# One decoder-trunk step on one core: the first loads and the modulation products in another order

## The chip, the cores and the metric

The kernel runs on one core of a Trainium2 chip. Its time is the device time of one execution in microseconds (us). TensorE (PE) multiplies and transposes, VectorE (DVE) and ScalarE (ACT) work on tiles, GpSimd (POOL) and SyncE (SP) here mostly issue DMAs.

## The reference

One inference step of a one-layer trunk, for a prompt of 1024 tokens and a sample group of 8 x 8 tokens (1088 tokens, width 1024). The part that matters here is its beginning, cut down:

```python
def post_norm_layer(x, c, w_mod_l, b_mod_l, ...):
    m = (jax.nn.silu(c) @ w_mod_l + b_mod_l).reshape(B, 6, 1, D)
    sh1, sc1, g1, sh2, sc2, g2 = [m[:, i] for i in range(6)]
    mix_out, new_state = mix_fn(x * (1 + sc1) + sh1)      # split_proj(h @ w_in), pooling, gating, attention
    x = layer_norm(ALPHA * x + (1 + g1) * mix_out, ln_g_l[0], ln_b_l[0])
    h2 = x * (1 + sc2) + sh2
    ff = moe(h2, router_w, router_b, wg, wu, wd)
    return layer_norm(ALPHA * x + (1 + g2) * ff, ln_g_l[1], ln_b_l[1]), new_state
```

The modulation `silu(c) @ w_mod` has six vectors of 1024 for each of nine rows of c. The first two (sh1, sc1) are needed before anything can be projected; the other four only after the projection. `rel_bias` gives a table of biases by distance, used by the attention.

## The kernel before

**Blocks.** The program is a sequence of blocks with a barrier between them: projection and compression (`block_projection`), attention, output projection, routing, experts, combination. Inside a block each engine has its own list of instructions, written out by hand, and semaphores (`wait_ge`) order the engines. Nothing schedules at run time. Only `block_projection` is changed.

**Modulation.** `w_mod` is 24 MB. It is loaded in twelve halves, 0 to 11 (`mod_load`, 2048 KB each; half n is rows 4*(n%2) to +3 of vector n//2). Halves 0 to 3 have buffers of their own. Halves 4 to 11 share one buffer, so that the load of half n waits until the products of half n-1 are done (`mod_half_done`), and the first of them waits until the weights of stage B, which lie in the same memory, have been split (`w_lo`). `mod_products(n)` (L329) is 16 fp32 multiplications with 32 output rows each, 32 records in the trace. `mod_vector` (DVE) adds the bias; `modulation_turn` (L620) transposes a finished vector, and a copy by DVE (L1042) puts it into `modT`, which every tile of x needs.

**Tiles of x.** There are nine: eight of 128 tokens and one of the 64 sample tokens. Two buffers are used in turn, so that `load_x(i)` waits for the transposes of tile i-2 (`xT_ready`). `transposes(i)` (L656) are eight PE transposes; ACT (`h_part`) and DVE (`h_values`) apply scale and shift, and the result is split into a high and a low fp32r part (L824, L826, L941).

**Stages.** PE runs `natural(n)` for n = 0 to 26 (L673): stage A (n = 0 to 8, 384 columns of `w_in`), stage B (n = 9 to 17, 408 columns), stage C (n = 18 to 26, 256 columns), tile n%9 each. The weights of a stage are loaded raw, then split into parts by ACT (L808) and DVE (L914). In stage A the transposes of tile i+2 follow `natural(i)`. `keys` (L684) and `gating` (L696) are small PE steps between them. Eight `group`s (L713) follow. `MOD_AFTER` says after which n the products of halves 4 to 11 stand.

**Bias table.** PE and DVE make a table of 8 rows by 1152. ACT stores it (L838) to DRAM sixteen times over, 8 x 16 x 1152 fp32, for loads much later.

**SP's queue** is in order: a load that waits holds every load behind it. It issues the halves, the tiles of x, the weights, and thirteen small loads (L496, L499, L500: scales, norms, pool state, page table and others; `small_in`, `pe_in`). `keep_busy` (L90) is a row of PE transposes of the identity without use for the result.

Of the kernel before, what the change touches and what calls it, by code (L numbers as in the profile page):

```python
# [30 lines left out]
KT = D // P  # L31
# [3 lines left out]
NT = NP_TILES + 1  # L35
# [3 lines left out]
PW = 256  # L39
WINDOWS = (2, 4, 8, 16)  # L40
PBUF = 15
HD, NKV, REP, NH = 64, 2, 4, 8
# [334 lines left out]
WIDTHS = (384, 408, 256)  # L377
CUTS = (3 * P, 3 * P, NP_TILES * P + NS - 6 * P)
N_GROUPS_T = 8
MOD_AFTER = {NT + 2: 4, NT + 4: 5, NT + 6: 6, NT + 8: 7, 2 * NT + 2: 8, 2 * NT + 4: 9, 2 * NT + 6: 10, 2 * NT + 8: 11}  # L380


def projection_weights(c):
# [32 lines left out]
def block_projection(c):  # L416
# [2 lines left out]
    projection_weights(c)  # L419
    c_n = c.view(MIX_, D)  # L420
    onehot, relb = c.view(KT_, TABW), c.view(KT_ + TABW, NH)
    tab = c.view(VS_, TABW)
    sgu_n = c.view(KVR_, 4, P)
    consts = c.view(CPH_, P + 2 * NS)
    trilT, blk64, rep8 = consts[:, 0:P], consts[:, P:P + NS], consts[:, P + NS:]
# [35 lines left out]
    with nc.Block() as block:  # L461
        @block.sync
        def _(sp):
# [9 lines left out]
            def load_w(n, at, width, dst, ks=slice(0, KT)):  # L473
                sp.dma_start(dst[:, ks, :], w_src[:, ks, at:at + width]).then_inc(c.w_in_in[n], 16)

            for n in range(3):
                mod_load(c, sp, n)
            load_x(0)
            mod_load(c, sp, 3)
            for h in range(2):  # L480
                load_w(h, KV0, WIDTHS[0], c.w_raw[0], slice(4 * h, 4 * h + 4))
            load_x(1)
            load_x(2)
            sp.wait_ge(w_lo, A_UNITS)
            load_w(2, KV0 + WIDTHS[0], WIDTHS[1], c.w_raw[1])
            load_x(3)
            for dst, src in (
                (c.pool_sc, bass.AP(tensor=t["pool_scale"].tensor, offset=0, ap=[[1, P], [P, 2]])),
                (c.lnv_g, row_broadcast(t["sgu_ln_g"], 0, PW)),
# [8 lines left out]
                lo = HD * (g % 2)  # L498
                sp.dma_start(c.sgu_b[lo:lo + HD, g // 2, :], row_broadcast(t["sgu_b"], g * P, P, HD)).then_inc(small_in, 16)  # L499
            sp.dma_start(c.pe_n[0:32, :], t["cmp_pe"][0].rearrange("s (c q) d -> (s c) (q d)", q=2)).then_inc(c.pe_in, 16)  # L500
            for i in range(4, NT):
                load_x(i)
            load_w(3, 2 * PW, PW, c.w_raw[2])
            sp.dma_start(share.rearrange("p m t -> p (m t)"), t["share"]).then_inc(share_in, 16)
            sp.wait_ge(w_lo, FIRST_UNIT[2])
            for n in range(4, 8):
                mod_load(c, sp, n)
            sp.wait_ge(z_ready, 2 * NT)
            sp.wait_ge(w_lo, GROUP_UNIT)
            load_w(4, 0, 512, c.pu_raw)  # L510
            for n in range(8, 12):
                mod_load(c, sp, n)
            sp.wait_ge(z_ready, 3 * NT)
            load_w(5, Q0, 512, c.q_raw)
# [92 lines left out]
        def _(pe):  # L607
# [52 lines left out]
            def natural(n):  # L660
                st, i = n // NT, n % NT
                T, at = tile_rows(i), i * P
                if n >= 2:
                    pe.wait_ge(*((z_act, n - 1) if n - 2 < 2 * NT else (z_dve, n - 1 - 2 * NT)))
                hi, lo = c.w_parts[st]
                units = (A_UNITS, B_UNITS, C_UNITS)[st]
                for k in range(KT):
                    if st == 0 and k % 4 == 0:
                        pe.wait_ge(h_lo, 2 * i + 1 + k // 4)
                    if i == 0 and k * units % KT == 0:  # L670
                        pe.wait_ge(w_lo, FIRST_UNIT[st] + k * units // KT + 1)
                    for left, right in ((0, hi), (0, lo), (1, hi)):
                        mm = pe.matmul(stage_bank(n)[0:T, 0:WIDTHS[st]], h_parts[left][:, k, at:at + T], right[:, k, :],  # L673
                                       start=(k == 0 and left == 0 and right is hi), stop=(k == KT - 1 and left == 1))
                mm.then_inc(z_ready, 1)
# [75 lines left out]
            bias_table()  # L751
            mod_products(c, pe, 1)
            gate_weights()
            keep_busy(c, pe, 7, 12)
            mod_products(c, pe, 2)
            sample_gate_weights()
            keep_busy(c, pe, 3, 16)
            mod_products(c, pe, 3)
            for v in range(2):
                modulation_turn(v)  # L760
            transposes(0)
            transposes(1)
            for n in range(3 * NT):
                st, i = n // NT, n % NT
                natural(n)
# [8 lines left out]
            for n in range(N_GROUPS_T):  # L774
                group(n)
                if n == 0:
                    gating(smp)
                if n == 1:
                    buffer_turn()
                if n == 4:  # L780
                    natural_pool()
                if n == 5:
                    pool_mix(0)
                if n == 6:
                    pool_mix(1)
# [5 lines left out]
        def _(act):  # L791
# [42 lines left out]
            act.dma_start(consts, t["cph1"]).then_inc(cph1_in, 16)  # L834
            act.wait_ge(c_in, 32)
            act.activation(c_n[0:9, :], c_n[0:9, :], ACT.Silu).then_inc(silu_done, 1)
            act.wait_ge(tab_done, 1)
            act.dma_start(c.tab_d, tab[0:NH, :].unsqueeze(1).to_broadcast([NH, TROWS, TABW])).then_inc(c.tab_out, 16)  # L838
            for u in range(4):
                part_high(u)  # L840
            act.wait_ge(modT_done, 2)
# [4 lines left out]
            for n in range(2 * NT):  # L846
                st, i = n // NT, n % NT
                T, s = tile_rows(i), i % 2
                z = stage_bank(n)
                act.wait_ge(z_ready, n + 1)  # L850
                if st == 0:
                    if i >= 2:
                        act.wait_ge(kv_out[s], 16 * 2 * (i // 2))
                        act.wait_ge(kT_ready, i - 1)
                    act.copy(kv_a[s][0:T, :], z[0:T, 0:WIDTHS[0]]).then_inc(z_act, 1)
                    if i + 2 < NT:
                        h_part(i + 2)
                    if 3 <= i < 3 + B_UNITS:
                        part_high(FIRST_UNIT[1] + i - 3)
                    continue  # L860
                if i >= 2:
                    act.wait_ge(kT_ready, n - 1)
                if i >= 6:
                    act.wait_ge(win_out[s], 16 * ((i - 4) // 2))
                if i == 0:
                    act.wait_ge(c.tab_out, 16)
                act.copy(c.vs[0:T, i, :, :, :].rearrange("p b g d -> p b (g d)"),
                         z[0:T, 0:512].rearrange("p (b w) -> p b w", b=2)[:, :, 0:P])
                act.copy(kv_b[s][0:T, :], z[0:T, P:2 * P])
                act.copy(c.gates[0:T, i, :], z[0:T, 3 * P:3 * P + 24]).then_inc(z_act, 1)  # L870
                if i in (3, 4):
                    part_high(FIRST_UNIT[2] + i - 3)
# [30 lines left out]
        def _(dve):  # L903
# [151 lines left out]
            for n in range(2 * NT):  # L1055
                st, i = n // NT, n % NT
                if st == 0 and i + 2 < NT:
                    h_values(i + 2)
                    for half in range(2):
                        h_low(i + 2, half)  # L1060
                if n >= 1:
                    keys_out(n - 1)
                if st == 0 and 3 <= i < 3 + B_UNITS:
                    part_low(FIRST_UNIT[1] + i - 3)
                if st == 1 and i in (3, 4):
                    part_low(FIRST_UNIT[2] + i - 3)
                if st == 1 and i == 5:
                    mod_vector(c, dve, 2)
            for i in range(NT):
                normed(i)  # L1070
                if i == 0:
                    keys_out(2 * NT - 1)
                if i >= 1:
                    gated(i - 1)
                if i == 1:
                    mod_vector(c, dve, 3)
                if i == 5:
                    mod_vector(c, dve, 4)
                if i in (6, 7):
                    part_low(GROUP_UNIT + i - 6)  # L1080
            for n in range(N_GROUPS_T):
                if n == 0:
                    mod_vector(c, dve, 5)
                    gated(smp)
                if n < 2:
                    for j, w in enumerate(CUTS):
                        pc = 3 * n + j
# [1819 lines left out]
```

## Time and profile before

| | |
|---|---|
| three runs, median | 1250.42 us (1245.3 to 1256.1) |
| profiled execution | 1253.85 us |
| its span in the trace | 1252.1 us |
| busy: PE, DVE, ACT | 1119.1, 731.7, 587.6 us |
| stage A on PE | 47.12 to 96.5 us |
| stage B on PE | 96.5 to 144.2 us |
| stage C on PE | to 188 us |
| granted PE clock, mean | 0.946 of full |

The profiled execution is 3.4 us over the median of the three runs. Times in a trace count from the start of the span. A row's bracket gives the idle time just before it and what ended it.

### The profile page before, as it was taken

The numbers are of one execution on the slowest core, as the hardware profiler recorded it, in microseconds if no ns is written. First come the engines' busy times: TensorE is split into PE (matmuls) and PEld (weight loads), VectorE is DVE, ScalarE is ACT, GpSimd is POOL, SyncE is SP. The second block draws the span as 40 slices with busy tenths as digits, with TensorE's granted clock in tenths as the row PEclk, the third lists the DMA queues.
The fourth block names the chain that finished last, engine by engine and source line by source line (L and its number), as shares of the span: only waits on it lengthen the run. The fifth ranks groups of instructions, "written<-read, shape, count | busy, mean of one in ns | idle before, by whom it ended". The sixth has DMA issues, their size and how long they took to land. (4 is left out here: it accounts for less than half of the span.)

```text
span 1252.1 us, 20501 instructions
## 1 busy us (share of the span) xinstructions
PE 1119.1 (89%) x7389; PEld 904.6 (72%) x7390; DVE 731.7 (58%) x1433; ACT 587.6 (47%) x1022; POOL 135.2 (11%) x203
## 2 busy tenths in 40 slices
PE   5699989998799999999889936999999999999844
PEld 3598879987666777778568725878888888888611
DVE  1461263243554777777676768885484588565157
ACT  0461100113465776766533235774475477555145
POOL 0212402010100000000000001020000011000061
PEclk9799999999997999999999967999999999999967
DMA  9645755054484300000343357996696599693488
GB/s 325 200 140 222 288 206 154 1 62 111 127 332 165 61 1 2 1 2 2 109 143 122 118 211 281 374 385 252 232 377 223 222 383 392 263 372 114 175 302 151
DMA packets 92343, 238.07 MB, mean 190 GB/s; under 512 B 8662, under 2 KB 18069, under 8 KB 92239
## 3 DMA queue, kind: packets, MB, share of 16 engines
q1 hardware_dynamic: 76153, 189.92, 43.2%
q0 software_dynamic: 10288, 31.20, 8.0%
q10 hardware_dynamic: 5830, 15.99, 3.6%
q8 instruction: 45, 0.74, 0.2%
q14 instruction: 27, 0.22, 0.1%
HBM read 199.04 MB, written 44.33 MB: 194 GB/s over the span
## 5 line engine op out<-in xcount | busy, mean ns | idle before, releaser
L2562 PE MATMUL psum<-w_hi,x_parts 128*128 128x512 f32 x736 | 239.7, 397 | 9.0 <-DVE x_parts L2681 9.0
L2674 DVE TENSOR_TENSOR w_lo<-raw,w_hi 128x2048 fp32r<-128x2048 f32 x95 | 213.3, 2286 | 44.7 <-ACT w_hi L2615 43.7
L2615 ACT CAST w_hi<-raw 128x2048 fp32r<-128x2048 f32 x90 | 167.6, 1914 | 29.3 <-DMA raw<-in_moe_w_gate 15.2
L2562 PEld LDWEIGHTS psum<-w_hi,x_parts 128*128 128x128 f32 x736 | 139.8, 190 | 39.8 <-issue 10.7
L2562 PE MATMUL psum<-w_lo,x_parts 128*128 128x512 f32 x368 | 144.7, 393 | 0.0
L2562 PE MATMUL psum<-w_hi,a_parts 128*128 x368 | 120.4, 399 | 4.0 <-DVE a_parts L2687 4.0
L1758 DVE CUSTOM_DVE_ANT_0 low<-psum,high 128x512 f32<-128x512 f32 (+5 forms) x172 | 92.2, 578 | 42.1 <-PE psum L1446 28.0
L1476 PE MATMUL psum<-keep,low 128*128 128x128 f32 (+1 forms) x556 | 95.0, 292 | 11.9 <-ACT high L1705 6.1
L1644 ACT ACTIVATE low<-low,high 128x640 f32<-128x640 f32 (+9 forms) x140 | 98.9, 709 | 9.9 <-DVE high L1758 9.6
L1671 ACT COPY high<-psum 128x512 f32<-128x512 f32 (+3 forms) x128 | 63.7, 502 | 81.5 <-PE psum L1476 81.3
L713 PE MATMUL psum<-h_hi,l_parts 128*128 128x384 f32 (+1 forms) x384 | 93.8, 327 | 0.0
L2037 PE MATMUL psum<-wo_parts,mix_parts 128*128 128x512 f32 x384 | 93.2, 399 | 0.0
L1476 PEld LDWEIGHTS psum<-keep,low 128*128 128x128 f32 (+1 forms) x556 | 60.9, 143 | 43.5 <-issue 28.7
L2037 PEld LDWEIGHTS psum<-wo_parts,mix_parts 128*128 128x128 f32 x384 | 72.1, 191 | 17.1 <-issue 2.1
L2562 PEld LDWEIGHTS psum<-w_hi,a_parts 128*128 128x128 f32 x368 | 69.8, 190 | 18.2 <-issue 4.2
L2562 PEld LDWEIGHTS psum<-w_lo,x_parts 128*128 128x128 f32 x368 | 69.8, 190 | 14.0
L1494 PE MATMUL psum<-high 128*64 128x128 f32 x1056 | 73.4, 283 | 0.0
L2562 PE MATMUL psum<-w_lo,a_parts 128*128 x184 | 72.2, 393 | 0.0
L713 PEld LDWEIGHTS psum<-h_hi,l_parts 128*128 128x128 f32 x384 | 67.4, 188 | 0.6 <-issue 0.4
L673 PE MATMUL psum<-l_parts,h_hi 128*128 128x384 f32 (+3 forms) x288 | 64.9, 316 | 1.5 <-DVE h_lo L941 1.3
L1446 PE MATMUL psum<-score_parts 64*128 64x512 f32 (+3 forms) x528 | 65.1, 371 | 0.0
L1494 PEld LDWEIGHTS psum<-high 128*64 128x64 f32 x1056 | 57.5, 139 | 10.4 <-issue 8.0
(384 smaller groups left out, 1734.6 us busy)
## 6 DMA issues: line engine op xcount, KB each, us to landing
raw<-in_moe_w_gate SPq DMA_DIRECT2D x16, 2048.0 KB, 11.5
raw<-in_moe_w_up SPq DMA_DIRECT2D x16, 2048.0 KB, 11.0
raw<-in_moe_w_down SPq DMA_DIRECT2D x16, 2048.0 KB, 10.8
top<-in_w_mod SPq DMA_DIRECT2D x8, 2048.0 KB, 8.0
y_d<-work ACTq DMA_DIRECT2D x24, 512.0 KB, 5.8
low<-in_w_mod SPq DMA_DIRECT2D x4, 2048.0 KB, 18.9
high<-in_x_prompt SPq DMA_DIRECT2D x16, 512.0 KB, 3.9
y_d<-high SPq DMA_DIRECT2D x1, 8192.0 KB, 23.8
```

Of the source, the lines that this page charges most:

```text
L673: mm = pe.matmul(stage_bank(n)[0:T, 0:WIDTHS[st]], h_parts[left][:, k, at:at + T], right[:, k, :], start=(k == 0 and left == 0 and right i ...
L713: mm = pe.matmul(piece_bank(pc)[:, 0:w], left[:, k, :], h_parts[right][:, k, toks], start=(k == 0 and left is hi and right == 0), stop=(k ...
L1446: mm = pe.matmul(c.bank(2 * g + q % 2)[:, 0:w * P], left[rows, j, :], right[rows, br, keys], start=n == 0, stop=n == 2)
L1476: mm = pe.transpose(turn_bank(what)[0:w, (k - 4 * m) * P:(k - 4 * m + 1) * P], pb[n % 3][:, g, k * P:k * P + w], c.ident)
L1494: mm = pe.matmul(c.bank(6 + br)[HD * g:HD * g + HD, j * P:(j + 1) * P], c.vs[:, k0 + k, br, g, :], pT[n % 2][:, g, k, :], start=(k == 0), ...
L1644: act.activation(x, x, ACT.Exp, bias=mx[:, at + g:at + g + 1], scale=-1.0, accum_out=sums[g]).then_inc(e_ev, 1)
L1671: act.copy(dst[:, 0:w], src[:, 0:w]).then_inc(r_act, 1)
L1758: dve.tensor_tensor_reduce(pb[n % 3][:, g, at * P:at * P + cols], c.bank(2 * g + q % 2)[:, 0:cols], bias, -1.0, least if m else 3e38, ALU. ...
L2037: mm = pe.matmul(c.bank(2 * (s % 2) + n), mixed[i % 2][l][:, k, :], wo[w][:, k, n * 512:(n + 1) * 512], start=(k == 0 and l + w == 0), sto ...
L2562: mm = pe.matmul(out, left[l][:, k * P:(k + 1) * P], w[:, bass.ds(at - o + k * step, 512)], start=n == 0, stop=n == len(steps) - 1)
L2615: act.copy(c.w_hi[:, at:at + PART // 2], c.raw[:, o:o + PART // 2]).then_inc(hi_done[p], 1)
L2674: dve.tensor_tensor(low, c.raw[:, o:o + PART // 2], c.w_hi[:, at:at + PART // 2].bitcast(F32), ALU.subtract).then_inc(c.lo_done[p], 1)
```

## The change

It does five things in `block_projection`, and moves no arithmetic.

1. SP's queue in the front: tile 0 of x is asked for before half 2, tile 1 between the two pieces of stage A's weights, and tiles 3 to 8 in a row. The thirteen small loads and `share` come after them, behind the load of stage C's weights.
2. The bias table is made in another place of SBUF, the memory of stage C's raw weights. Its store moves from the front of ACT's list to stage A, after `h_part(6)` (iteration i = 4). Therefore the load of stage C's weights now waits for `tab_out`, and a wait of ACT for it at the first tile of stage B is gone.
3. PE in the front: vector 0 is turned right after half 1, tile 0 is transposed after half 2, tile 1 in the middle of `natural(0)`. The rows of `keep_busy` are 12, 16 and then 24 long; before they were 12 and 16.
4. Products of halves 4 to 11: before after n = 11, 13, 15, 17, 20, 22, 24, 26; now after n = 9, 11, 13, 15, 17, 21, 24 and after group 0.
5. `mod_vector` 2, 3 and 5 on DVE are moved to follow them.

```diff
-MOD_AFTER = {NT + 2: 4, NT + 4: 5, NT + 6: 6, NT + 8: 7, 2 * NT + 2: 8, 2 * NT + 4: 9, 2 * NT + 6: 10, 2 * NT + 8: 11}
+MOD_AFTER = {NT: 4, NT + 2: 5, NT + 4: 6, NT + 6: 7, NT + 8: 8, 2 * NT + 3: 9, 2 * NT + 6: 10}
...
-    tab = c.view(VS_, TABW)
+    tab = c.view(MIX_ + 2 * KT * WIDTHS[1], TABW)
...
-            for n in range(3):
-                mod_load(c, sp, n)
+            mod_load(c, sp, 0)
+            mod_load(c, sp, 1)
             load_x(0)
+            mod_load(c, sp, 2)
             mod_load(c, sp, 3)
-            for h in range(2):
-                load_w(h, KV0, WIDTHS[0], c.w_raw[0], slice(4 * h, 4 * h + 4))
+            load_w(0, KV0, WIDTHS[0], c.w_raw[0], slice(0, 4))
             load_x(1)
+            load_w(1, KV0, WIDTHS[0], c.w_raw[0], slice(4, 8))
             load_x(2)
             sp.wait_ge(w_lo, A_UNITS)
             load_w(2, KV0 + WIDTHS[0], WIDTHS[1], c.w_raw[1])
-            load_x(3)
+            for i in range(3, NT):
+                load_x(i)
+            sp.wait_ge(c.tab_out, 16)
+            load_w(3, 2 * PW, PW, c.w_raw[2])
+            sp.dma_start(share.rearrange("p m t -> p (m t)"), t["share"]).then_inc(share_in, 16)
             for dst, src in (
...
-            for i in range(4, NT):
-                load_x(i)
-            load_w(3, 2 * PW, PW, c.w_raw[2])
-            sp.dma_start(share.rearrange("p m t -> p (m t)"), t["share"]).then_inc(share_in, 16)
             sp.wait_ge(w_lo, FIRST_UNIT[2])
-            for n in range(4, 8):
+            for n in range(4, 10):
                 mod_load(c, sp, n)
             sp.wait_ge(z_ready, 2 * NT)
             sp.wait_ge(w_lo, GROUP_UNIT)
             load_w(4, 0, 512, c.pu_raw)
-            for n in range(8, 12):
+            for n in range(10, 12):
                 mod_load(c, sp, n)
...
                 for k in range(KT):
+                    if n == 0 and k == 4:
+                        transposes(1)
...
             gate_weights()
-            keep_busy(c, pe, 7, 12)
+            modulation_turn(0)
+            sample_gate_weights()
+            keep_busy(c, pe, 3, 12)
             mod_products(c, pe, 2)
-            sample_gate_weights()
+            transposes(0)
             keep_busy(c, pe, 3, 16)
             mod_products(c, pe, 3)
-            for v in range(2):
-                modulation_turn(v)
-            transposes(0)
-            transposes(1)
+            modulation_turn(1)
+            pe.wait_ge(sguS_done, 1)
+            keep_busy(c, pe, 7, 24)
...
                     if i + 2 < NT:
                         h_part(i + 2)
+                    if i == 4:
+                        act.wait_ge(tab_done, 1)
+                        act.dma_start(c.tab_d, tab[0:NH, :].unsqueeze(1).to_broadcast([NH, TROWS, TABW])).then_inc(c.tab_out, 16)
```

PE in the front, from the products of half 1 to stage A. Where a line has two numbers, the first is the changed kernel's: L621/L620 turn a vector, L642/L641 make the sample's gate weights, L657/L656 transpose x. Before:

```order
L635 MATMUL psum<-keep,high 128x128 x3
L90 MATMUL psum<-keep 128x128 x12
L329 MATMUL psum<-low,top 32x256 [waits modw_in2]
L329 MATMUL psum<-low,top 32x256 x15
L641 MATMUL psum<-high 64x64 [waits sgu_done]
L641 MATMUL psum<-high 64x64 x3
L90 MATMUL psum<-keep 128x128 x16
L329 MATMUL psum<-low,top 32x256 [waits modw_in3]
L329 MATMUL psum<-low,top 32x256 x15
L620 MATMUL psum<-keep,top 128x128 [waits mods_ready]
```

The transposes of tiles 0 and 1 then stand before stage A. Now:

```order
L642 MATMUL psum<-high 64x64 x3
L90 MATMUL psum<-keep 128x128 x12
L329 MATMUL psum<-low,top 32x256 [waits modw_in2]
L329 MATMUL psum<-low,top 32x256 x15
L657 MATMUL psum<-keep,high 128x128 [waits tab_done,x_in0]
L657 MATMUL psum<-keep,high 128x128 x7
L90 MATMUL psum<-keep 128x128 x16
L329 MATMUL psum<-low,top 32x256 [waits modw_in3]
L329 MATMUL psum<-low,top 32x256 x15
L621 MATMUL psum<-keep,top 128x128 [waits mods_ready]
L621 MATMUL psum<-keep,top 128x128
L90 MATMUL psum<-keep 128x128 [waits sguS_done]
```

Between half 3 and stage A stand one turn and 24 transposes of the identity, where two turns and the 16 transposes of tiles 0 and 1 stood.

SP's queue in stage A and at the beginning of stage B. Before:

```order
L474 DMA top<-in_w_in 128x8x408 [waits w_lo]
L471 DMA high<-in_x_prompt 128x1024 [waits xT_ready]
L496 DMA high<-in_pool_scale 128x2x1
L496 DMA high<-in_sgu_ln_g 128x256
...
L500 DMA keep<-in_cmp_pe 32x128
L471 DMA high<-in_x_prompt 128x1024 [waits xT_ready] x4
L471 DMA high<-in_x_sample 64x1024 [waits xT_ready]
L474 DMA low<-in_w_in 128x8x256
L504 DMA high<-in_share 128x32
L314 DMA top<-in_w_mod 128x4x1024 [waits w_lo]
```

Now:

```order
L474 DMA top<-in_w_in 128x8x408 [waits w_lo]
L471 DMA high<-in_x_prompt 128x1024 [waits xT_ready] x5
L471 DMA high<-in_x_sample 64x1024 [waits xT_ready]
L474 DMA low<-in_w_in 128x8x256 [waits tab_out]
L491 DMA high<-in_share 128x32
L501 DMA high<-in_pool_scale 128x2x1
...
L505 DMA keep<-in_cmp_pe 32x128
L314 DMA top<-in_w_mod 128x4x1024 [waits w_lo]
```

The load of half 4 (the last row) now stands behind a wait for the table's store and behind all small loads.

PE in stage B, at the end of `natural(9)`. Before:

```order
L673 MATMUL psum<-b_parts,h_hi 128x408 x2
L673 MATMUL psum<-b_parts,h_lo 128x408
L684 MATMUL psum<-keep,high 128x64 [waits kT_evac,z_act]
L673 MATMUL psum<-b_parts,h_hi 128x408 [waits z_act]
L673 MATMUL psum<-b_parts,h_hi 128x408
```

Now:

```order
L676 MATMUL psum<-b_parts,h_lo 128x408
L687 MATMUL psum<-keep,high 128x64 [waits kT_evac,z_act]
L329 MATMUL psum<-top 32x256 [waits mods_ready,modw_in4]
L329 MATMUL psum<-top 32x256 x15
L676 MATMUL psum<-b_parts,h_hi 128x408 [waits z_act]
```

The two rows of L329 are the products of half 4; before they stood two tiles later.

## Rows read from the trace of the kernel before

**Rows 1.** The page, engines: busy time, share, instructions.

```profile
PE 1119.1 (89%) x7389; PEld 904.6 (72%) x7390; DVE 731.7 (58%) x1433; ACT 587.6 (47%) x1022; POOL 135.2 (11%) x203
```

**Rows 2.** Timeline of PE in the front: start, duration, instruction, [idle before].

```profile
19.50 1.47 PE L90 MATMUL psum<-keep 128*128 128x128 f32 x12
23.89 2.40 PE L329 MATMUL psum<-low,top 128*32 128x256 f32 x32 [2.91 <-DMA low<-in_w_mod]
27.27 3.67 PE L90 MATMUL psum<-keep 128*128 128x128 f32 x16
36.77 3.64 PE L329 MATMUL psum<-low,top 128*32 128x256 f32 x32 [5.83 <-DMA low<-in_w_mod]
47.12 0.62 PE L673 MATMUL psum<-l_parts,h_hi 128*128 128x384 f32 x2 [1.33 <-DVE h_lo L941]
51.85 1.03 PE L656 MATMUL psum<-keep,high 128*128 128x128 f32 x8
59.84 1.97 PE L656 MATMUL psum<-keep,high 128*128 128x128 f32 x8 [2.52 <-DMA high<-in_x_prompt]
```

**Rows 3.** Busy time in stretches; the share behind POOL's is the granted PE clock.

```profile
26.00:31.00 5.00, 4.94 (x28) 4.20 (x24) 0.42 (x1) 0.00 (x0) 0.00 (x0) 0.50 1.01 278
41.00:45.00 4.00, 3.34 (x17) 3.31 (x17) 1.60 (x6) 0.81 (x3) 2.05 (x4) 0.50 0.09 23
46.00:57.00 11.00, 9.67 (x56) 9.11 (x56) 9.74 (x22) 8.08 (x19) 4.27 (x9) 1.00 0.60 197
```

**Rows 4.** DMA totals of 0 to 24 and of 19 to 22.5 us.

```profile
DMA packets 2896, 8.04 MB, mean 335 GB/s; under 512 B 270, under 2 KB 1038, under 8 KB 2895
...
DMA packets 366, 1.43 MB, mean 408 GB/s; under 512 B 20, under 2 KB 20, under 8 KB 365
```

**Rows 5.** DMA by queue, 22.5 to 33.5 us (q10: ACT's), then 33.5 to 43 us.

```profile
q10 hardware_dynamic: 136, 0.59, 35.1%
...
q1 hardware_dynamic: 799, 1.80, 52.1%
```

**Rows 6.** Timeline: ACT's store of the table, DVE's copy of vector 1, ACT in tile 6.

```profile
18.51 0.87 ACTq L838 DMA_DIRECT2D tab_d<-high  x1
...
42.42 0.23 DVE L1042 COPY keep<-psum 128x72 f32<-128x72 f32 x1 [0.78 <-PE psum L620]
...
79.91 0.62 ACT L826 CAST h_hi<-high 128x512 fp32r<-128x512 f32 x1
```

**Rows 7.** Timeline of SP's queue in stage A.

```profile
52.13 0.43 SPq L496 DMA_DIRECT2D high<-in_pool_scale  x1
...
60.15 12.84 SPq L471 DMA_DIRECT2D high<-in_x_prompt  x4
...
78.35 0.59 SPq L474 DMA_DIRECT2D low<-in_w_in  x1
```

**Rows 8.** DMA issues of 50 to 56, 92 to 102 and 112 to 121 us: KB, us to landing.

```profile
high<-in_x_prompt SPq DMA_DIRECT2D x1, 512.0 KB, 8.4
...
top<-in_w_mod SPq DMA_DIRECT2D x1, 2048.0 KB, 9.1
...
top<-in_w_mod SPq DMA_DIRECT2D x1, 2048.0 KB, 7.6
```

**Rows 9.** Timeline of PE at the end of `natural(9)`.

```profile
101.13 0.27 PE L684 MATMUL psum<-keep,high 64*128 64x64 f32 x1
```

**Rows 10.** Waits of PE from 90 to 300 us: total, times, longest.

```profile
PE psum L329 <- DMA top<-in_w_mod: 4.5, 4, 1.8
```

**Rows 11.** Timeline of PE and DVE at the end of stage C.

```profile
187.47 0.66 PE L696 MATMUL psum<-high 128*64 128x128 f32 x8
188.75 1.93 PE L329 MATMUL psum<-top 128*32 128x256 f32 x32 [0.63 <-DMA top<-in_w_mod]
190.62 0.62 PE L713 MATMUL psum<-h_hi,l_parts 128*128 128x384 f32 x2
...
189.52 0.54 DVE L974 TENSOR_SCALAR high<-psum,high 64x256 f32<-64x256 f32 x1
```

More of the change, by code:

```diff
@@ L777, in _ @@
                     gating(smp)
+                    mod_products(c, pe, 11)
                 if n == 1:
@@ L836, in _ @@
             act.activation(c_n[0:9, :], c_n[0:9, :], ACT.Silu).then_inc(silu_done, 1)
-            act.wait_ge(tab_done, 1)
-            act.dma_start(c.tab_d, tab[0:NH, :].unsqueeze(1).to_broadcast([NH, TROWS, TABW])).then_inc(c.tab_out, 16)
             for u in range(4):
@@ L864, in _ @@
                     act.wait_ge(win_out[s], 16 * ((i - 4) // 2))
-                if i == 0:
-                    act.wait_ge(c.tab_out, 16)
                 act.copy(c.vs[0:T, i, :, :, :].rearrange("p b g d -> p b (g d)"),
@@ L1066, in _ @@
                     part_low(FIRST_UNIT[2] + i - 3)
-                if st == 1 and i == 5:
+                if st == 1 and i == 4:
                     mod_vector(c, dve, 2)
+                if st == 1 and i == 8:
+                    mod_vector(c, dve, 3)
             for i in range(NT):
@@ L1074, in _ @@
                     gated(i - 1)
-                if i == 1:
-                    mod_vector(c, dve, 3)
                 if i == 5:
@@ L1082, in _ @@
                 if n == 0:
+                    gated(smp)
+                if n == 1:
                     mod_vector(c, dve, 5)
-                    gated(smp)
                 if n < 2:
```

## The prediction

> **What bounds the kernel now.** I read the page's engines first: PE is busy 89% of the span [rows 1], so what counts is where PE stands idle or at half clock, and the change touches only the first 200 us. Then PE's timeline in the front. It waits 2.91 us for half 2 of the modulation and 5.83 us for half 3, stage A begins at 47.12, and PE waits once more, 2.52 us, for tile 3 of x at 59.84 [rows 2]. The clock comes next: at half from 26 to 31 and from 41 to 45, full from 46 [rows 3]. After 60 us nothing is idle on PE until stage C, where it waits four times for a half, 4.5 us in all [rows 10]. So the block is a late start, one gap in stage A, four small ones in stage C, and otherwise back-to-back PE work. The changed kernel does the same PE work plus 24 transposes of the identity.
>
> I make the sum against the profiled execution, 1253.85 us, and set it off against the median of 1250.42, 3.4 us lower, at the end.
>
> **Why half 3 is late.** ACT issues the table's store at 18.51 [rows 6]. Its 0.59 MB take 35.1% of sixteen engines for 11 us [rows 5], which is 62 engine-us, against 1.43 MB in 3.5 us at 408 GB/s (56 engine-us for more than twice the bytes) just before [rows 4]. And once it is through, from 33.5 to 43 us, the loads use only 52.1% of the engines [rows 5]: about half of them have finished, and the other half still owe what they could not move while they stored the table. A load has landed when its slowest engine has.
>
> **Front, with the store gone.** By 24 us 8.04 MB were moved [rows 4]. Up to and with half 3 the queues carry four halves (8.4 MB), tile 0 (0.5) and about 0.8 MB of constants, 9.7 in all. The table had some 0.2 MB of the 8.04, so that 1.9 MB are left, 4.7 us at 408 GB/s: half 3 lands at about 28.7 and not at 36.8. Tile 0 now goes ahead of half 2 and delays it by 0.52 MB, 1.3 us: 25.2.
>
> PE then runs half 2, eight transposes of tile 0, 16 of the identity, half 3, one turn. At full clock these are 1.93 [rows 11], 1.03, 16/12 of 1.47 [rows 2], then 1.93: half 3 is begun at 30.1 and done at 32.0. At half clock they are 3.64, 1.97, 3.67 and 3.64 [rows 2]: done at 38.1. From the end of half 3's products to DVE's copy of vector 1 (42.42 to 42.65 [rows 6]) the old kernel took 2.2 us with two turns, the new one needs about 1.7. From that copy to stage A it took 4.5 us, of which 1.5 went to waiting for tile 0's transposes, which are now done before: 3.0. Stage A would start at 36.7 at full clock. The gap before half 2 is 2.5 us or so, and after gaps of 2.91 and 2.52 us the old kernel was at half clock [rows 2, 3]. [...] Gain **8.1** (7 to 10.4).
>
> **Tile 3 of x.** Its load lands 8.4 us after issue, in the company of 1632 KB of weights and small loads [rows 8]. Without the small ones (0.6 MB up to there) it lands 1 to 1.4 us earlier against the start of stage A, and PE arrives 1.03 us later, since the transposes of tile 1 now stand in `natural(0)` [rows 2]. Of the 2.52 us 0 to 0.5 are left, the clock doesn't fall, and the transposes at 59.84 cost 1.03 and not 1.97. Against it stand the 1.03 of tile 1. Gain **2.1** (1.5 to 2.5). Tiles 4 to 8 were not waited for before and are now asked for earlier.
>
> **The new wait in stage B.** The load of half 4 is now the last of a chain on SP. Count from ACT's cast of tile 6, behind which the store is issued: 79.91 in old time [rows 6], called T. The store took 11 us of transfer and at most 15.0 from issue to the end (18.51 to 33.5 [rows 5, 6]); with an idle queue I take 12.5 (11 to 15). Then SP issues stage C's weights and `share`, 1.2 us at 0.6 each, and the thirteen small loads, 8.0 us (52.13 to 60.15 [rows 7]): T+21.7. A half then needs 7.6 to 9.1 us [rows 8], I take 8.2: **T+29.9**. PE asks for it behind `keys(8)`, 101.4 in old time [rows 9], T+21.5. So PE waits **8.4** us (6 to 12), and since both ends hang on the same tile this doesn't depend on what the front gains. Behind the wait on PE stand all of stages B and C; nobody fills in. After so long a gap PE is at half clock: at least the products cost 3.64 and not 1.93, 1.7 us; at most it lasts as from 36.77 to 45.7, 9 us at half, 4.5 us. I take **2.5**. The other small costs have cover: the weights of stage C are asked for at T+12.5 and used in tile 12 of stage B, over 20 us later; the stores of k and v share the table's engines until T+12.5, and the first copy that waits for one of them is due about then.
>
> The Trainium skill (SBUF — State Buffer, on Door 1, the DMA port swizzle, with the port rate of DMA: Bandwidth & Descriptors, Where 436 GB/s comes from) lets eight neighbouring partitions reach only two of the sixteen ports, which for 0.59 MB gives an estimate of 10.8 us wherever the store stands; by that rule the 11 us of the row stay with it in stage A.
>
> **Products after that.** Half n is loaded once n-1 is done, 7.6 to 9.1 us; products two tiles of stage B apart are over 11 us apart, so no further wait. In stage C there are two products where there were four, three and four tiles apart: three waits go, 3.9 of the 4.5 us. The fourth was 0.63, at 188.75, and half 11's products stood there; now group 0 comes straight away, but it waits for DVE's `z_dve`, 189.52 + 0.54 = 190.06, against PE free at 188.13 [rows 11]. PE thus idles 1.9 us where wait and products took 2.5, and pays the products, 1.9 us, after group 0: 1.3 lost. Gain in stage C **2.5** (2 to 3.5). The page loads, behind product 11 on SP, start some 12 us later and are used over 60 us later.
>
> **Sum.** -8.1 - 2.1 + 8.4 + 2.5 - 2.5 = -1.8: 1252.0 for the profiled execution, **1249** against the median. Own range: -8 to +5, 1242 to 1255. Everything behind the block only shifts.
>
> **Rivals.**
> 1. *The table's store is cheap where it stands now*, with no other load in its way, or SP's small loads go out faster: no wait in stage B, clock kept. For it: alone, it may not need 11 us. Against: half 4 would have to be asked for 14 us after T, and 9.2 us of issues alone lie before it. -12.7: 1238. Chance 0.12.
> 2. *Slower: PE stays at half clock through the front.* Place: PE between half 2 and stage A, where 24 transposes of the identity now stand. For it: from 26 to 31 us PE was busy almost throughout, 16 such transposes among it, and stayed at 0.50 [rows 3]. Against: it was at 0.50 from 41 to 45 with the transposes of tiles 0 and 1 and at 1.00 from 46 [rows 3]. Price: half 3 done at 38.1, turn at 39.4, the 24 at 3.67/16 each 5.5 us, stage A at 44.9 and not 39, part of it given back at tile 3: +5.3, 1254. It decides from a start of stage A later than 41, where the gain of the front no longer pays the wait in stage B. Chance 0.13. The Trainium skill (TensorE: Matmul & The Clock Gate, Part 4: PE-mode transpose) says that transposes don't count as activity that lifts the clock. By that rule rival 2 is what happens; the rows from 41 to 57 us speak against it.
> 3. *The change doesn't do what it says in the front*: half 3 lands at 36.8 as before, because something else held it. Stage A at 43.5 to 45; the rest as above: +3.5, 1252.5. The half-idle engines [rows 5] speak against it. Chance 0.08.
>
> **How the numbers follow.** Forecast 0.67, rivals 0.12, 0.13, 0.08. About 1%, 12.5 us, is what a measurement of this kernel tells from no change; the forecast and rivals 2 and 3 lie within it. Faster by more: most of rival 1 at its edge, 0.08. Slower by more: rival 2 together with the upper bounds of the wait, 0.05. The range is 1239 to 1257.
>
> **What the changed kernel's profile would show.** Half 3's products begin at 30 to 34.5 us; stage A at 36.7 to 40; the row of PE for tile 3 with under 0.5 us of idle; one wait of PE of 6 to 12 us for the load of half 4 after `natural(9)`, with half clock behind it; no wait at L329 in stage C. The prediction is wrong if that wait is missing or if stage A begins after 41.

## The result and the profile after

The changed kernel took **1255.11 us** (median of 20 runs, 1250.83 to 1258.35), the kernel before 1248.01 (20 runs). The ratio is 1.0049, 95% interval 1.0035 to 1.0064: 6.1 us slower by the ratio (7.1 by the medians). The forecast was 1249, within a microsecond or so of no change.

The two profiled executions hide this (spans 1252.1 and 1253.1 us), because the one of before ran 21 us of its attention block at half clock and the one of after did not. Busy time in 373 to 394 us, of before, then of after; the share behind POOL's is the granted clock:

```profile
373.00:394.00 21.00, 21.00 (x159) 12.76 (x148) 7.74 (x34) 9.14 (x32) 0.61 (x1) 0.51 0.49 160
```

```profile
373.00:394.00 21.00, 20.27 (x231) 13.77 (x232) 10.14 (x43) 13.28 (x47) 0.61 (x1) 1.00 0.70 224
```

So places in the program are compared, not spans. PE's timeline of the kernel after, front to first group (start, duration, instruction, [idle before]):

```profile
23.89 1.93 PE L329 MATMUL psum<-low,top 128*32 128x256 f32 x32 [1.41 <-DMA low<-in_w_mod]
26.69 1.91 PE L90 MATMUL psum<-keep 128*128 128x128 f32 x16
30.46 1.93 PE L329 MATMUL psum<-low,top 128*32 128x256 f32 x32 [1.86 <-DMA low<-in_w_mod]
33.22 2.78 PE L90 MATMUL psum<-keep 128*128 128x128 f32 x24
37.06 0.62 PE L676 MATMUL psum<-l_parts,h_hi 128*128 128x384 f32 x2 [1.06 <-DVE h_lo L945]
...
49.55 1.09 PE L657 MATMUL psum<-keep,high 128*128 128x128 f32 x8 [1.84 <-DMA high<-in_x_prompt]
...
84.86 0.61 PE L676 MATMUL psum<-b_parts,h_hi 128*128 128x408 f32 x2
...
107.83 3.22 PE L329 MATMUL psum<-top 128*32 128x256 f32 x32 [18.06 <-DMA top<-in_w_mod]
...
193.94 0.59 PE L716 MATMUL psum<-h_hi,l_parts 128*128 128x384 f32 x2 [2.08 <-DVE high L978]
```

Against [rows 2], stage A starts 10.1 us earlier and half 3 lands at 30.4 us instead of 36.7. Stage B begins at 84.86, in the kernel before at 96.50:

```profile
96.50 0.61 PE L673 MATMUL psum<-b_parts,h_hi 128*128 128x408 f32 x2
```

That is 11.6 us of lead. One wait of 18.06 us, for half 4, takes it and more. The first group starts at 193.94 and not at 190.62 [rows 11], 3.3 us late, and product 11 (1.93 us) is still to come. From stage B's start to the first group the kernel needs 15.0 us more: 18.06 of wait, +1.3 for the product at half clock, -4.5 for stage C's old waits [rows 10], -1.9 for product 11, +2.1 for the wait on DVE in the last row. The pool step, in both the same wait of PE on ACT, shows what then remains. After, then before:

```profile
270.44 3.45 PE L748 MATMUL psum<-high 64*64 64x512 f32 x12 [2.07 <-ACT high L899]
```

```profile
265.28 2.05 PE L745 MATMUL psum<-high 64*64 64x512 f32 x12 [2.07 <-ACT high L895]
```

It starts 5.2 us late and takes 1.4 us more, because in this execution the clock falls at that point (0.61 granted from 270 to 274 us): 6.6 us, against 6.1 measured.

**Why 18 us.** The queues of ACT, SP and POOL in the kernel after, in order of time:

```profile
67.76 0.87 ACTq L863 DMA_DIRECT2D tab_d<-low  x1
...
81.97 0.38 SPq L474 DMA_DIRECT2D low<-in_w_in  x1
...
87.42 0.60 POOL L587 DMA_DIRECT2D out_o_win_s<-in_state_win_kv  x1
...
90.60 20.91 SPq L314 DMA_DIRECT2D top<-in_w_mod  x2
```

The chain that I had worked out is there: 14.2 us for the table's store (12.5 foreseen), 8.6 us of issues (9.2 foreseen). New is the third row: GpSimd's copy of the window state, one array of device memory to another. Now it is 3 us ahead of half 4; in the kernel before it stood 7 us behind it (half 4 issued at 92.30):

```profile
99.05 0.60 POOL L586 DMA_DIRECT2D out_o_win_s<-in_state_win_kv  x1
```

DMA issues and queues in 90.6 to 108 us (KB, us to landing; the row DMA is the busy share of sixteen engines in 40 slices, in tenths):

```profile
DMA  0392999585599595977030234455555555420000
q1 hardware_dynamic: 804, 2.21, 34.1%
q0 software_dynamic: 65, 1.65, 23.5%
top<-in_w_mod SPq DMA_DIRECT2D x1, 2048.0 KB, 17.2
```

Half 4 needs 17.2 us from issue to landing, against the 7.6 to 9.1 of [rows 8]. From 98 to 106 us the engines are at most half busy (share 0.38, then 0.49), while half 4 has still not landed: the picture that [rows 5] gave of the table's store.

### The profile page after: what moved, and what is told of

It is laid out like the page before. It is cut to its first block and busy times, and to the rows that moved or that the text cites. A ratio compares the mean times of both kernels' runs of the same rounds, so it can differ in the third digit from the quotient of the medians.

```text
span 1253.1 us, 20548 instructions
## 1 busy us (share of the span) xinstructions
PE 1110.9 (89%) x7413; PEld 898.9 (72%) x7414; DVE 731.8 (58%) x1433; ACT 587.6 (47%) x1022; POOL 135.7 (11%) x203
## 5 line engine op out<-in xcount | busy, mean ns | idle before, releaser
L1649 ACT ACTIVATE low<-low,high 128x640 f32<-128x640 f32 (+9 forms) x140 | 98.9, 710 | 11.1 <-DVE high L1763 10.9
```

Of the source, the lines that this page charges most:

```text
L1649: act.activation(x, x, ACT.Exp, bias=mx[:, at + g:at + g + 1], scale=-1.0, accum_out=sums[g]).then_inc(e_ev, 1)
```

## The experiments

Ratios are against the kernel before, run beside each. "Wait" is PE's for half 4 and half 5 in stage B, from the profiled execution; "group 0" is the start of the first group there.

| kernel | median us | ratio (95%) | wait 4 / 5 | group 0 |
|---|---|---|---|---|
| before | 1248.0 | 1 | 0 / 0 | 190.6 |
| changed | 1255.1 | 1.0049 (1.0035 to 1.0064) | 18.1 / 0 | 193.9 |
| copy late | 1248.4 | 0.9987 (0.9966 to 1.0007) | 8.4 / 0 | 187.4 |
| half 4 first | 1249.9 | 0.9999 (0.9981 to 1.0017) | 0.3 / 9.2 | 187.0 |
| both | 1237.1 | 0.9892 (0.9866 to 0.9919) | 0 / 2.4 | 180.5 |
| store early | 1253.8 | 1.0036 (1.0013 to 1.0059) | 0 / 5.9 | 191.5 |
| copy, b c e | 1255.1 | 1.0044 (1.0024 to 1.0065) | 17.3 / 0 | 193.3 |
| before + places | 1254.8 | 1.0045 (1.0023 to 1.0067) | 0 / 6.6 | 193.7 |
| front only | 1250.0 | 1.0011 (0.9987 to 1.0034) | 9.4 / 0 | 190.2 |
| both, half 5 too | 1236.0 | 0.9886 (0.9855 to 0.9917) | 0 / 0.2 | 174.9 |
| copy in 62 | 1269.9 | 1.0153 (1.0123 to 1.0184) | 17.8 / 5.2 | 210.4 |
| before + places, copy late | 1245.8 | 0.9976 (0.9954 to 0.9998) | 0.5 / 0 | 185.0 |
| before, copy late | 1246.9 | 0.9973 (0.9952 to 0.9993) | 0 / 0 | 192.9 |
| the same again | 1251.2 | 1.0008 (0.9977 to 1.0039) | 0 / 0 | 191.4 |
| half 5 too, old places | 1239.3 | 0.9909 (0.9873 to 0.9944) | 0 / 0 | 180.7 |
| copy in 32 | 1255.0 | 1.0042 (1.0009 to 1.0074) | 13.9 / 0 | 193.0 |
| half 5 too, copy in 32 | 1237.5 | 0.9899 (0.9867 to 0.9932) | 0 / 0 | 176.1 |

Waits and group 0 are of one execution each, and those of copy late (1264.3 us) and of both (1241.5 us) are the longest of their kernels: in both of them stage B starts 1.9 us later than in the changed kernel's.

**Copy late.**

```diff
-            pool.dma_start(t["o_pool_s"][0, :, 0:PBUF - JS, :], t["state_pool"][0, :, JS:PBUF, :]).then_inc(c.out_done, 16)
-            pool.dma_start(t["o_win_s"][0, :, 0:PAST - JS].rearrange("b s a g d -> b (s a g d)"),
-                           t["state_win_kv"][0, :, JS:PAST].rearrange("b s a g d -> b (s a g d)")).then_inc(c.out_done, 16)
-            c.out_total += 32
...
             pool.dma_start(t["o_sgu_s"][0].rearrange("b j w -> (b j) w"), c.vn[smp % 2][0:NS, :]).then_inc(sgv_out, 16)
+            (the same four lines)
```

> The changed kernel with one edit: GpSimd's two copies from one array of device memory to another (pool state and window state, 1984 KB in eight long rows) are issued behind the last store of stage C, at about 192 us, instead of at 87.4 us. Theory (the copy stretched the landing of half 4): half 4, asked for at about 90.6 us, lands in 8 to 9 us instead of 17.2, TensorE's wait for it in stage B falls from 18.1 us to about 9, and the time falls by 8 to 10 us against the changed kernel, to about 1246 us. Rival (the landing is slow because of the table's store and the small loads of stage C's weights ahead of it on SyncE): the landing stays at 16 to 18 us and the time within 2 us of the changed kernel. Second rival: the copy has to be somewhere, and costs the same between 192 and 205 us, where half 11 or stage C's outputs are moved: wait gone in stage B, new one of 5 us or more behind it.

Half 4 was issued at 92.16. PE's timeline, then the DMA issues from 90 to 103 us:

```profile
100.06 3.64 PE L329 MATMUL psum<-top 128*32 128x256 f32 x32 [8.44 <-DMA top<-in_w_mod]
```

```profile
top<-in_w_mod SPq DMA_DIRECT2D x1, 2048.0 KB, 7.9
```

The landing falls from 17.2 to 7.9 us and the wait to 8.44, the 8.4 of the prediction. By the ratios the edit is worth 0.6%, 7.7 us. Both rivals fall: from 190 to 300 us PE waits for no half. (The profiled execution had 47 us at half clock in its attention block; only its first 200 us are used.)

**Half 4 first**, and **both** edits together.

```diff
+            sp.wait_ge(w_lo, FIRST_UNIT[2])
+            mod_load(c, sp, 4)
             sp.wait_ge(c.tab_out, 16)
...
-            sp.wait_ge(w_lo, FIRST_UNIT[2])
-            for n in range(4, 10):
+            for n in range(5, 10):
```

> The changed kernel with one edit: SyncE asks for half 4 as soon as its buffer is free, before it waits for the table's store and issues stage C's weights and small rows. Theory (chain of table store, 14.2 us, and SyncE's issues, 8.6 us, holds half 4 back, and the copy then stretches it): half 4 is issued near 80 us and landed near 88.5, TensorE asks for it at 89.7 and waits for nothing; half 5 then is the one behind the chain and beside the copy, issued near 91.8, landed near 107, asked for at about 101, wait 5 to 7 us. Time 11 to 13 us below the changed kernel, about 1242 us. Rival (half 4 is late for a reason of its own: its buffer or its own size): wait for half 4 stays above 8 us and the time moves by less than 4 us.

> The changed kernel with both edits: half 4 asked for first, and the two copies behind stage C's last store. Theory: no wait of TensorE for halves 4 or 5 in stage B; the time is 17 to 20 us below the changed kernel, about 1236 us, which would be 11 to 12 us below the kernel before. Rival (the waits of stage B are cover for something that ends as late, such as VectorE's work between stages): stage B is shorter but the first group starts at the same point, and the time falls by less than 10 us.

Half 4 first: its wait is gone, but half 5 is waited for 9.2 us, not 5 to 7, and the gain is 6 us, half of what I expected. I had looked for half 5 beside the copy; it isn't. It is issued only at 104.00 and lands in 8.0 us. SP's timeline shows what holds it (start, duration of the issues):

```profile
91.19 0.23 SPq L503 DMA_DIRECT2D page<-in_page_table  x1
91.46 8.92 SPq L503 DMA_DIRECT2D high<-in_pool_w  x2
100.43 2.90 SPq L506 DMA_DIRECT2D high<-in_sgu_b  x4
103.37 0.59 SPq L507 DMA_DIRECT2D keep<-in_cmp_pe  x1
104.00 0.42 SPq L314 DMA_DIRECT2D top<-in_w_mod  x1
```

Two issues that take 1.31 us in the changed kernel take 8.92. Without the copy there (both), the same two take 1.31 again, half 5 is issued at 95.81, and 2.4 us of wait are left. From stage C's weights to the next half SP's issues take 8.6 us in the changed kernel, 12.0 in both and 20.4 here: half 4 ahead of them makes part of it, the copy the larger part. So the copy holds a load back either on the engines or through the issues ahead of it. What such a long issue waits for, the trace doesn't show. Both edits together take 19.6 us off the changed kernel by the ratios, more than the 7.7 and 6.2 of each alone, since each alone leaves the other's wait.

**Store early.** The table's store is back at the front of ACT's list.

```diff
+            act.wait_ge(tab_done, 1)
+            act.dma_start(c.tab_d, tab[0:NH, :].unsqueeze(1).to_broadcast([NH, TROWS, TABW])).then_inc(c.tab_out, 16)
...
-                    if i == 4:
-                        act.wait_ge(tab_done, 1)
-                        act.dma_start(c.tab_d, tab[0:NH, :].unsqueeze(1).to_broadcast([NH, TROWS, TABW])).then_inc(c.tab_out, 16)
```

> The changed kernel with the table's store back at the front of ScalarE's list, as in the kernel before, and all else as changed. Theory (the store beside half 3 costs the front, the store at 67.8 us costs stage B): half 3 lands near 36.7 us instead of 30.4, stage A begins 4 to 6 us later than in the changed kernel; SyncE no longer waits for the table at 82 us, half 4 is issued before the copy, and the wait for it falls from 18.1 us to 0 to 2 us, with 0 to 6 us for half 5. Sum: 8 to 13 us below the changed kernel, about 1244 us. Rival (only the copy's place matters, it hits whichever half is in flight): half 4's or half 5's wait is still above 8 us and the time is within 5 us of the changed kernel.

PE's timeline, half 3 and half 5:

```profile
38.04 3.35 PE L329 MATMUL psum<-low,top 128*32 128x256 f32 x32 [6.68 <-DMA low<-in_w_mod]
...
115.58 3.64 PE L329 MATMUL psum<-top 128*32 128x256 f32 x32 [5.87 <-DMA top<-in_w_mod]
```

Half 3 at 38.0 and stage A at 45.6: of the front's gain the store's place makes 8.6 us, the order of x and the turns the rest. Half 4 isn't waited for, and now it is half 5 that the copy catches (15.1 us from issue to landing). Both waits are as the theory had them (0 to 2 and 0 to 6; the rival wanted over 8), but the time is not: stage A starts 8.6 us later and not 4 to 6, and the time is only 1.6 us below the changed kernel's, not 8 to 13. What theory and rival share is shown: while the copy stands in stage B it hits the half in flight.

**The parts by themselves**: the new places in the kernel before, and the changed kernel with the old places. The first edit is this, with SP's ranges and `mod_vector` 2, 3 and 5 as in the change; the second is its reverse.

```diff
-MOD_AFTER = {NT + 2: 4, NT + 4: 5, NT + 6: 6, NT + 8: 7, 2 * NT + 2: 8, 2 * NT + 4: 9, 2 * NT + 6: 10, 2 * NT + 8: 11}
+MOD_AFTER = {NT: 4, NT + 2: 5, NT + 4: 6, NT + 6: 7, NT + 8: 8, 2 * NT + 3: 9, 2 * NT + 6: 10}
```

> The kernel before with one part of the change: the new places of halves 4 to 11 (and the vectors that go with them), with the old order of the x tiles and the table's store in front. By the prediction's rows: three waits of stage C are gone, 2.5 us net, and stage B gets none of the 8.4 us that come with the table's store; half 4, issued near 92.3 us, is asked for near 101. Theory from the changed kernel's trace (GpSimd's copy, issued near 99 us, hits the half that is then in flight, here half 5): 5 to 7 us of wait for half 5, so the time is 2 to 5 us above the kernel before. Rival (the places are harmless by themselves): no wait over 1 us in stage B, time 2 to 3 us below the kernel before.

> The changed kernel with the old places of halves 4 to 11 (half 4 behind n = NT + 2, the last behind 2 NT + 8), so the front and the table's store as changed and nothing else. Theory: TensorE asks for half 4 two units later, near 99.5 us; it lands near 107.8 under the copy, wait 8 to 9 us, and stage C has its old waits of 3.9 us. Front 10 us earlier, tile 3 of x 1.6 worse... sum -10 + 1.6 - ... + 8.5: the time is within 2 us of the kernel before, about 1248 us, 6 to 7 us below the changed kernel. Rival (the earlier front itself moves later work into waits that have nothing to do with half 4): above 1252 us.

The places alone cost 0.45%, as much as the whole change. PE's timeline of that kernel:

```profile
118.40 3.64 PE L329 MATMUL psum<-top 128*32 128x256 f32 x32 [6.62 <-DMA top<-in_w_mod]
```

The front alone is no faster than before: its 10 us go into a wait of 9.35 for half 4. Every gain ahead of that load was a wait for it.

**How the copy delays a load.** Three forms of it at its old place: on both sides of the copy this, and then `c b e` in place of `b c e`, with c=62 and with c=32.

```diff
-.rearrange("b s a g d -> b (s a g d)")
+.rearrange("b s a g d -> b (s a g d)").rearrange("b (c e) -> b c e", c=62)
```

> The changed kernel with the window-state copy at its place (87.4 us) but cut into 62 pieces of 4 KB a row, 496 in all, instead of eight rows whose packets are 63,488 bytes and lie on 8 of the 16 DMA engines. Theory (half 4 is stretched because its share on those 8 engines stands behind long packets while the other 8 are done at 98.9): with the copy on all 16 engines half 4 and the copy, 2 MB each, end together near 100 to 103 us, and TensorE's wait falls from 18.1 us to 11 to 13; time 4 to 7 us below the changed kernel, about 1249 us. Rival (only the bytes count, not how they lie): half 4 still lands near 106 to 108 us, and the time is within 2 us of the changed kernel's 1255.

> The changed kernel with the window-state copy walked the other way round: 62 pieces of 4 KB, each for all eight rows, before the next (c b e instead of b c e; with b c e the profile still showed 32 packets of 63,488 bytes). Theory (half 4 stands behind long packets on 8 of the 16 DMA engines): packets are now 4 KB and lie on all 16, the copy and half 4 end together near 100 to 103 us, TensorE's wait falls from 18.1 to 11 to 13 us, time 4 to 7 us below the changed kernel. Rival (the bytes alone count): half 4 lands at 106 to 108 us as before and the time stays at the changed kernel's. Second rival (4 KB pieces from one array of device memory to another move slower, and every queue pays): half 4 lands later than 108 us.

> The changed kernel with the window-state copy at its place (87.4 us) in 32 outermost pieces, each of 7,936 bytes from all eight rows. The copy in eight outermost rows held about 8 engines (DMA share 0.49 while it and half 4's late half remained), the one in 62 pieces about 2 of 16 (share near 0.1, 59.6 us). The Trainium skill (DMA: Bandwidth & Descriptors, Why a DMA increments its semaphore by 16 and not by 1) says that the number of engines is the largest one up to 16 that divides the outermost size: 8 for 8, 2 for 62, and 16 for 32. Theory (the spread counts): copy and half 4 share all engines, 4.1 MB at the 400 GB/s or so of the rows make 10 us after 90.6, so half 4 lands at 101 to 103.5 us, TensorE's wait falls from 18.1 to 11.5 to 14 us; time 4 to 7 us below the changed kernel's 1255. Rival (bytes and order count, not the spread): landing at 106 us or later, time as the changed kernel's.

The first changes nothing, neither packets (32 of 63,488 bytes as before) nor time: it is a repeat of the changed kernel, 1.0044 beside 1.0049, and says nothing on its theory. With 62 pieces outermost I expected all sixteen engines; the copy took 59.6 us at a share of 0.1. The copy among the DMA issues of that kernel, the DMA row there from 112 to 150 us, and the copy in the changed kernel:

```profile
out_o_win_s<-in_state_win_kv POOLq DMA_DIRECT2D x1, 1984.0 KB, 59.6
```

```profile
DMA  1179999961111211111118799995311114311110
```

```profile
out_o_win_s<-in_state_win_kv POOLq DMA_DIRECT2D x1, 1984.0 KB, 15.0
```

Between the halves the share is that of one or two engines of sixteen, and PE waits for halves 4, 5 and 6 (17.8, 5.2, 4.3 us): 19 us slower than before by the ratio. With 32 outermost the copy takes 10.9 us and half 4 lands in 12.6, at 105.3 us and not at 101 to 103.5, since it is issued 2.1 us later. DMA issues and PE's timeline:

```profile
top<-in_w_mod SPq DMA_DIRECT2D x1, 2048.0 KB, 12.6
```

```profile
105.41 3.64 PE L329 MATMUL psum<-top 128*32 128x256 f32 x32 [13.93 <-DMA top<-in_w_mod]
```

Shares of 8, 2 and 16 engines, as the Trainium skill (DMA: Bandwidth & Descriptors, Why a DMA increments its semaphore by 16 and not by 1) has it with the largest divisor up to 16 of the outermost size, fit all three. The trace agrees as far as it goes: it names no engine, but 59.6 us is four times 15.0. So the same bytes cost half 4 9.3 us beside eight engines and 4.7 beside sixteen (17.2 and 12.6, less the 7.9 without the copy). The packets changed too, from 63,488 bytes to 7,936, and what each did isn't separated; with 62, in packets of 4 KB on few engines, half 4 still took 16.9 us. In the time this gain isn't seen (1.0042): group 0 starts only 0.9 us earlier in the profiles, because half 4 was issued 2.1 us later, after a fall of the clock in stage A that the changed kernel's profile lacks, and the half clock behind the wait took 1.4 us more. The interval, 0.33% either way, leaves room for the 4 us expected and for none.

**Controls and the fastest version.**

```diff
             load_w(3, 2 * PW, PW, c.w_raw[2])
+            mod_load(c, sp, 5)
             sp.dma_start(share.rearrange("p m t -> p (m t)"), t["share"]).then_inc(share_in, 16)
...
-            for n in range(5, 10):
+            for n in range(6, 10):
```

That is "half 5 too", on top of both edits. The other kernels here combine edits already shown.

> The kernel before with one edit: the two copies behind stage C's last store. A control: there half 4 landed at 101.4 us and was asked for at 110.7, so the copy at 99 us stood in nobody's way. Theory: no difference above 1 us, which shows that the gain of the same edit in the changed kernel is that of half 4's wait. Rival (the copy's place is worth something in any order, or costs something at 190 us, where stage C's loads and stores are): 2 us or more either way.

> The kernel before with the two copies behind stage C's last store, once more, word for word the kernel that gave 0.9973 [0.9952, 0.9993]. Theory (no wait is touched; the difference was chance in where TensorE's clock falls in the attention block): ratio within 0.9985 to 1.0015. Rival (the late copy gains by itself): 0.996 to 0.9985 again.

> The kernel before with the new places of halves 4 to 11 and the two copies behind stage C's last store, so that nothing is beside half 5. With the copy at its old place the same kernel took 1254.8 us and waited 6.6 us for half 5. Theory (the places are worth the 2.5 us that the prediction gave them; the copy alone turned them into a loss): wait for half 5 below 1 us, time 7 to 9 us less, 1246 to 1247.5 us, 2 to 3 us below the kernel before. Rival (the places gain nothing, since the first group waits for VectorE's last unit of stage C instead): within 1 us of the kernel before.

> Built on the kernel with half 4 asked for first and the two copies behind stage C's last store (1237.1 us, where half 5, issued at 95.8 us behind the small rows, was still waited for 2.4 us, and its product took 3.6 us at the half clock): half 5 is now asked for ahead of the small rows, as soon as half 4's product has freed the buffer, near 93.6 us. Theory: it lands by 102 us, no wait, its product 1.9 us at the full clock; time 2 to 4 us less, 1233 to 1235 us. Rival (the small rows for stage C, now 11 us later, or VectorE's work at stage B's end become the last to arrive): no change or slower than 1237 us.

> The fastest kernel so far (halves 4 and 5 asked for early, the copies late, 1236.0 us) with the old places of halves 4 to 11: the last of them in stage C again. Theory: halves 4 and 5 are not waited for; stage C has the four short waits of the kernel before (0.4 to 1.8 us each), so the first group starts 2 to 3 us later than at 174.9 us and the time is 1238 to 1239 us. Rival (VectorE ends stage C and covers those waits): within 1 us of 1236.

> The fastest kernel (1236.0 us: halves 4 and 5 asked for early, the copies behind stage C's last store) with the late copy in 32 outermost pieces. Theory (nobody waits for what stands beside the copy there): within 2 us of 1236. Rival (half 11 or the first group's weights wait behind it unseen): 2 us or more faster.

In the kernel before, the late copy gave 0.9973 and, the second time, 1.0008. The two intervals overlap, and in both profiles group 0 starts no earlier than before: the gain of 0.3%, though its interval is clear of 1, did not come again and was most likely chance. An effect of the copy there of 0.2% isn't excluded. The new places beside a late copy are 0.69% (8.6 us) better than beside the early one, and stand where the control of the same chip does (0.9976 and 0.9973); with intervals of 0.2% either way, a 2.5 us gain of the places can't be told from none there. In the fastest kernel PE is without a gap for most of stage B (busy time in 90 to 170 us), and its twin with the old places waits for four halves (waits of PE from 90 to 300 us):

```profile
90.00:170.00 80.00, 79.70 (x679) 68.47 (x672) 27.30 (x77) 10.98 (x39) 19.12 (x37) 1.00 0.65 226
```

```profile
PE psum L329 <- DMA top<-in_w_mod: 4.2, 4, 1.9
```

It is 14 us below the kernel before (0.9886), but only 1 us below both, where 2 to 4 were expected: the ratios' intervals overlap almost wholly. The places are worth 0.23%, 2.9 us, of the 14, by ratios whose intervals overlap. Spreading the late copy gains nothing.

## Why the prediction was wrong

- **The step that failed** is in "The new wait in stage B": "A half then needs 7.6 to 9.1 us [rows 8], I take 8.2". It needed 17.2. Those rows of before are landings with the copy behind the half or absent; the change pulls half 4 back on SP's queue and, as ACT and PE run 11 us earlier, POOL's copy forward, and the two change places. I followed SP's queue and ACT's list and not POOL's, which no line of the diff touches. With 7.9 in its place (copy late) the wait was 8.44. That this is the forecast's 8.4 is in part luck: the chain took 22.5 us for 21.7, the load 7.9 for 8.2, and PE asked 22.0 us after the store's issue, not 21.5 after T. The 18.1 lies outside the wait's own 6 to 12; the stated range of 1239 to 1257 holds the result only because it is wide.
- **Chain ahead of the load:** right. 14.2 and 8.6 us against 12.5 and 9.2.
- **Front:** right in mechanism, low in size: 10.1 us against 8.1, within the 7 to 10.4. Half 3 landed at 30.4 (28.7 foreseen), and PE held the full clock. The 8.1 puts stage A at 39, with a part of the front at half clock; no run shows that. In all eleven runs with this front the granted clock was 1.00 from 24 to 49 us, and stage A started at 36.8 to 37.4, beside the 36.7 worked out for full clock. In four of them full speed came only at 23 to 24 us and half 2's products began at 26.4 to 26.6; stage A started at 37.2 to 37.4 all the same.
- **Rivals:** rival 2 (half clock through the front) didn't happen in any of the runs with this front, though 24 transposes of the identity stand right before stage A; what is said there of transposes isn't borne out by them. Rival 3 (half 3 as late as before) fell as well: store early shows that it was the store. Its price was too low by its own terms: stage A at 43.5 to 45 is 4.5 to 6 us behind 39, not 3.5. Rival 1 (no wait) was furthest off.
- **Tile 3 of x:** 1.6 us of lead against 2.1, and for another reason: 1.84 us of idle stayed (0 to 0.5 foreseen). The load took 8.2 us and landed 12.5 us after the start of stage A, against 12.7 before, where I had counted on 1 to 1.4 less. The gain is 0.7 us of idle and 1.35 from the full clock behind it (0.9 in the transposes, the rest after them), less 0.45 more on the way there (1.03 foreseen for tile 1). Copy late lost the clock there (50.9 to 54.4 us), and its stage B began 1.9 us later.
- **Half clock behind the wait:** the products took 3.22 and not 1.93, 1.3 us, where I took 2.5.
- **Stage C:** the three waits went, the wait on DVE (2.1 us) and product 11 behind group 0 came as foreseen. 2.4 us (4.5 less 2.1) against the 2.5 of the sum.

With the wait at 18.1 instead of 8.4, the front at -10.1, tile 3 at -1.6, half clock at +1.3 and stage C at -2.4 the same sum gives +5.3 against the 6.1 measured.

## What to carry over

Before pricing a load at the time it took elsewhere, list what every queue, those of untouched engines too, has in flight beside it in the new order: an engine that runs ahead pulls its own transfers forward. Here a load landed only when the engines that it shared with the copy were done, long after the others, and the same bytes cost it 9.3 us on eight engines and 4.7 on sixteen; put such a copy where nobody waits for a load. And when several gains end in one wait, none of them shows until that wait is gone: front and places made +6 us beside the early copy, and -14 with the copy late and halves 4 and 5 asked for early.

## What was not expected of the hardware

- The outermost size of a copy's access pattern decides how long 1984 KB take, as the number of engines would have it: 15.0 us with 8 outermost rows, 59.6 with 62, 10.9 with 32, and splitting it inside the row changed nothing.
- Issuing itself can take long: two issues of 1.31 us took 8.92 while the copy was in flight. The cause isn't shown.
- TensorE came to full speed at about 15 us in some runs and at 23 to 24 in others, with the same instructions ahead of it: half 1's products took 1.93 us from 17.0 on in the changed kernel and 3.64 from 18.8 on in copy late. The profile's granted clock reads 1.00 in both, and reads 1.00 too where half 0's products took 3.64 us (11.2 us in the changed kernel), so that in the first 24 us the durations have to be read.
